# One decoder step on one core: an attention sum, a core's front and the DVE order moved, a K=100 product in place of two of four rows, and output products in two column halves

## The reference

```
block 1: u = rmsnorm(x) @ w_in
         o_a = rwkv7(u_rwkv)            # 8 heads of 64, a state recurrence over the tokens
         o_b = diff_attention(u_attn)   # 4 heads: softmax(q1 k1) - lam * softmax(q2 k2), times v, then
                                        # o * rsqrt(mean(o*o)) over the head's 128 columns
         x += (g_a * (o_a @ w_a) + g_b * (o_b @ w_b)) @ w_out
         x += relu(rmsnorm(x) @ w_ff1)^2 @ w_ff2 ; x += (p @ w_ple) * sigmoid(rmsnorm(x) @ w_ple_gate)
block 2: linear attention, 4 heads of 128 x 256, chunks of 64 tokens:
         o = (q k^T, causal in the chunk) v + q S      # S: the state at the chunk's start
         dilated attention, 3 groups x 4 heads, each with out_g and lse_g:
         w_g = softmax over g of lse_g ; o = sum_g w_g * out_g
         then gates, out projection, MLP and the per-layer embedding as in block 1
```

## Time and profile before

| | |
|---|---|
| three runs | 1974.45, 1980.01, 1980.01 us; median 1980.01 |
| the profiled execution | 1975.9 us, span 1974.1 |
| PE busy | 1933.8 us, 98% |
| DVE, ACT, POOL busy | 50%, 39%, 15% |
| mean granted clock of PE | 0.994 of full |
| transfers | 185.70 MB, mean 94 GB/s |

### The profile page before, as it was taken

The page is one execution under the profiler, slowest core; times in us unless marked ns, Lnnn a source line. Parts: engine busy times, 40 slices in busy tenths (PEclk is TensorE's granted clock), DMA queues, the critical chain, the costliest instruction groups (busy, mean ns, idle before and its releaser), DMA issues.

```text
span 1974.1 us, 27695 instructions
## 1 busy us (share of the span) xinstructions
PE 1933.8 (98%) x11560; PEld 1576.5 (80%) x11560; DVE 978.8 (50%) x1550; ACT 777.8 (39%) x1260; POOL 289.0 (15%) x281
## 2 busy tenths in 40 slices
PE   8989999999999999999999999999999999999997
PEld 6866777778888888887787888887888888888886
DVE  6655766657432333367645344447533432333365
ACT  6555323244443332346333333344222443232345
POOL 1001233302210010122000000004201210010124
PEclk9999999999999999999999999999999999999999
DMA  5122111135233322234312122222222242223221
GB/s 198 64 69 70 66 55 61 56 123 186 82 117 118 109 96 99 93 107 136 110 54 71 68 75 86 77 84 75 96 96 95 88 150 96 98 95 102 93 94 54
DMA packets 60080, 185.70 MB, mean 94 GB/s; under 512 B 6595, under 2 KB 11843, under 8 KB 59828
## 3 DMA queue, kind: packets, MB, share of 16 engines
q1 hardware_dynamic: 59956, 183.94, 27.7%
HBM read 173.69 MB, written 10.22 MB: 93 GB/s over the span
## 4 chain that ended last, share of the span: by engine, by line
PE 84%; DVE 7%; ACT 4%; issue 2%; POOL 2%; DMA 1%; SPq 0%; DVEq 0%; POOLq 0%; ACTq 0%
PE P L571 25%; PE P L573 24%; PE P L572 24%; DVE AREN L1763 2%; POOL AREN L2497 1%; DVE AREN L1766 1%; DVE WLO L1770 1%; ACT WHI L1171 1%; ACT AREN L1475 1%; PE P L1100 1%; PE P L1066 1%; PE P L760 1%; PE P L907 1%; PE P L919 0%; PE P L923 0%
## 5 line engine op out<-in xcount | busy, mean ns | idle before, releaser
L571 PE MATMUL P<-HH,WHI 128*128 128x512 f32 x1528 | 614.3, 402 | 5.3 <-DVE HL L1783 3.4
L573 PE MATMUL P<-HH,WLO 128*128 128x512 f32 x1528 | 597.6, 391 | 0.0
L572 PE MATMUL P<-HL,WHI 128*128 128x512 f32 x1528 | 596.9, 391 | 0.0
L1171 ACT ACTIVATE WHI<-RAW 128x1024 fp32r<-128x1024 f32 x302 | 318.1, 1054 | 432.5 <-PE P L573 431.6
L1770 DVE TENSOR_TENSOR WLO<-RAW,WHI 128x1024 fp32r<-128x1024 f32 x302 | 376.7, 1248 | 146.2 <-ACT WHI L1171 144.7
L571 PE MATMUL P<-ARR,WHI 128*128 128x512 f32 (+1 forms) x920 | 353.3, 384 | 0.0
L572 PE MATMUL P<-ARR,WHI 128*128 128x512 f32 (+1 forms) x920 | 352.8, 384 | 0.0
L573 PE MATMUL P<-ARR,WLO 128*128 128x512 f32 (+1 forms) x920 | 352.8, 384 | 0.0
L571 PEld LDWEIGHTS P<-HH,WHI 128*128 128x128 f32 x1528 | 287.8, 188 | 77.3 <-issue 7.9
L573 PEld LDWEIGHTS P<-HH,WLO 128*128 128x128 f32 x1528 | 287.6, 188 | 61.9
L572 PEld LDWEIGHTS P<-HL,WHI 128*128 128x128 f32 x1528 | 288.2, 189 | 55.8 <-issue 0.2
(11 more groups left out here) (311 smaller groups left out, 1444.2 us busy)
## 6 DMA issues: line engine op xcount, KB each, us to landing
RAW<-in_w_in_dram SPq DMA_DIRECT2D x117, 512.0 KB, 3.3
RAW<-in_w_ff_dram SPq DMA_DIRECT2D x64, 512.0 KB, 3.3
RAW<-in_w_ml_dram SPq DMA_DIRECT2D x64, 512.0 KB, 3.3
RAW<-in_w_out_dram SPq DMA_DIRECT2D x16, 512.0 KB, 3.3
RAW<-in_w_pg_dram SPq DMA_DIRECT2D x16, 512.0 KB, 3.3
AREN<-in_xT_dram SPq DMA_DIRECT2D x16, 256.0 KB, 6.0
s_gates<-AREN SPq DMA_DIRECT2D x16, 256.0 KB, 2.0
RAW<-in_w_ab_dram SPq DMA_DIRECT2D x8, 512.0 KB, 3.3
```

Of the source, the lines that this page charges most:

```text
L571: e.matmul(out, hi, H[0][:, s], start=first, stop=False)
L572: e.matmul(out, hi, H[1][:, s], start=False, stop=False)
L573: return e.matmul(out, lo, H[0][:, s], start=False, stop=last)
L1171: e.activation(WHI[n % NSPL][:, :], RAW[n % NRAW][:, :], ACT.Copy).then_inc(*D.act.sig("whi", n))
```

## The change

Five edits. `ss` of head h-1 now stands behind `aw` of head h (rows 77, 103, 129). front(0)'s first chunk moves to rows 182, 189, 192, 194, and front(1)'s to 196, 200, 203, 205. DVE's add to Q moves, for levels 1 to 4, from the `c` streams to the `e` streams, so that DVE's order after an `lb` is T0, T1, Q0, Q1. Linear attention does all 8 score products of a head first (one wait for both banks), then the 14 state products, each cut in two of 64 weight columns that write the two halves of the partitions. The log sums are turned by f32 transposes; the two fp32r parts lie in one buffer at partitions 0 to 3 and 96 to 99, the rest of which POOL sets to zero in the `l` stream, and EYE has a second copy of the identity at rows 96 to 99, so that one product of K=100 does what two of K=4 did.

```diff
     for h in range(4):
...
-            out += [("pv", h - 1, 0)] if h and i == 1 else [("ss", h - 1, 0)] if h and i == 5 else []
+            out += [("pv", h - 1, 0)] if h and i == 1 else []
             out.append(("qk", h, i))
         out.append(("aw", h, 0))
+        out += [("ss", h - 1, 0)] if h else []
...
-        put("a", r, r, r, *((r,) if late else ()), r + 3, r + 3, r + 3, *((r + 3,) if late else ()), r + 6, r + 6,
-            r + 11, *((r + 13,) if r < 117 else ()), r + 21, r + 21, r + 21, r + 21)
+        put("a", r, r, r, *((r,) if late else ()), r + 3, r + 3, r + 3, r + 6, r + 6, r + 11,
+            *((r + 12,) if late else ()), *((r + 13,) if r < 117 else ()), r + 21, r + 21, r + 21, r + 21)
...
-    for jj, rows in ((0, (174, 178, 181, 184)), (1, (196, 199, 202, 205))):
+    for jj, rows in ((0, (182, 189, 192, 194)), (1, (196, 200, 203, 205))):
...
-        EYE = sb("EYE", 4, F32R, 4)
+        EYE = sb("EYE", 4, F32R)
...
-        dLS = [(arr(28 + g)[0:4, :], arr(31 + g)[0:4, :]) for g in range(3)]
+        dLS = [(arr(28 + g)[0:4, :], arr(28 + g)[96:100, :]) for g in range(3)]
...
+                    w.wait_ge(G.dve.at("at", h, 1), G.dve.at("s", h, 7), free.get(4), free.get(5))
                     for vb in range(2):
...
+                            for x, rw in enumerate(rws):
+                                d = e.matmul(bank(4 + vb)[rw, 64 * c:64 * c + 64],
+                                             gST[:, c, 128 * vb + 64 * x:128 * vb + 64 * x + 64],
+                                             q[:, 64 * c:64 * c + 64], start=False, stop=c == 7)
...
-                        d = e.matmul(o[0:4, 128 * qb:128 * qb + 128], LSE[:, 16 * g + 4 * qb:16 * g + 4 * qb + 4],
-                                     ident, start=True, stop=True)
+                        d = e.transpose(o[0:4, 128 * qb:128 * qb + 128], LSE[:, 16 * g + 4 * qb:16 * g + 4 * qb + 4], ident)
...
-                        for i_ in range(2):
-                            d = e.matmul(o, EYE[0:4, h:h + 1].to_broadcast([4, 128]), dLS[g][i_], start=i_ == 0,
-                                         stop=i_ == 1)
+                        e.matmul(o, EYE[0:100, h:h + 1].to_broadcast([100, 128]), arr(28 + g)[0:100, :], start=True,
+                                 stop=True).then_inc(*L.pe.sig("mix", h, g))
...
+                    if what == "lb" and lev < 5:
+                        add(Qm, Qm, o0[:, 128:384]).then_inc(*C.dve.sig("Q", q, lev))
...
-                        add(Qm, Qm, o0[:, 128:384] if lev < 5 else o0[:, 0:256]).then_inc(*C.dve.sig("Q", q, lev))
+                        else:
+                            add(Qm, Qm, o0[:, 0:256]).then_inc(*C.dve.sig("Q", q, 5))
...
+                w.wait_ge(L.pe.at("pv", 11), L.act.at("pt", 11, 0))
+                for g in range(3):
+                    e.memset(arr(28 + g).bitcast(F32), 0.0).then_inc(*L.pool.sig("lz", g))
```

More of the change, by code:

```diff
@@ L1056, in gla @@
                         yield
+                    w.wait_ge(G.dve.at("at", h, 1), G.dve.at("s", h, 7), free.get(4), free.get(5))
                     for vb in range(2):
[L1058 to L1061, removed]
                         for tb in range(4):
-                            e.matmul(o[:, 128 * tb:128 * tb + 128], gVT[:, tb, cs], gATv[:, tb, :], start=tb == 0,
-                                     stop=False)
+                            e.matmul(bank(4 + vb)[:, 128 * tb:128 * tb + 128], gVT[:, tb, 128 * vb:128 * vb + 128],
+                                     gATv[:, tb, :], start=tb == 0, stop=False)
+                    for vb in range(2):
                         for c in range(1, 8):
-                            d = e.matmul(o[:, 64 * c:64 * c + 64], gST[:, c, cs], q[:, 64 * c:64 * c + 64],
-                                         start=False, stop=c == 7)
+                            for x, rw in enumerate(rws):
+                                d = e.matmul(bank(4 + vb)[rw, 64 * c:64 * c + 64],
+                                             gST[:, c, 128 * vb + 64 * x:128 * vb + 64 * x + 64],
+                                             q[:, 64 * c:64 * c + 64], start=False, stop=c == 7)
                         d.then_inc(*G.pe.sig("o", h, vb))
-                        free[b] = G.dve.at("o", h, vb)
-                        yield
+                        free[4 + vb] = G.dve.at("o", h, vb)
+                    yield
+                    yield
                     b, o = take(G.pool.at("sq", h))
@@ L1151, in dilated @@
                     for g in range(3):
-                        b, o = take(L.dve.at("ls", g), K.pool.at("eye"))
-                        for i_ in range(2):
-                            d = e.matmul(o, EYE[0:4, h:h + 1].to_broadcast([4, 128]), dLS[g][i_], start=i_ == 0,
-                                         stop=i_ == 1)
-                        d.then_inc(*L.pe.sig("mix", h, g))
+                        b, o = take(L.dve.at("ls", g), K.pool.at("eye", 1))
+                        e.matmul(o, EYE[0:100, h:h + 1].to_broadcast([100, 128]), arr(28 + g)[0:100, :], start=True,
+                                 stop=True).then_inc(*L.pe.sig("mix", h, g))
                         free[b] = L.dve.at("mix", h, g)
@@ L1734, in dilated @@
                     yield
-                w.wait_ge(L.dve.at("lw"))
+                w.wait_ge(L.dve.at("lw"), L.pool.at("lz", 2))
                 for g in range(3):
@@ L2525, in begin @@
                 e.tensor_copy(ONES[:, :], cst("ones")).then_inc(*K.pool.sig("one"))
-                e.tensor_copy(EYE[:, :], ident[0:4, 0:4]).then_inc(*K.pool.sig("eye"))
+                e.memset(EYE[:, :].bitcast(F32), 0.0).then_inc(*K.pool.sig("eye0"))
+                w.wait_ge(K.pool.at("eye0"))
+                for i, at in enumerate((0, 96)):
+                    e.tensor_copy(EYE[at:at + 4, :], ident[at:at + 4, at:at + 4]).then_inc(*K.pool.sig("eye", i))
+                w.wait_ge(K.pool.at("eye", 1))
                 for i in range(2):
```

## The result

The changed kernel takes 1960.87 us (median of four runs, 1960.29 to 1965.27), the kernel before, in the same rounds, 1978.48 (1974.45 to 1980.01). The ratio is 0.9919, with a 95% interval of 0.9897 to 0.9941: it is faster. Its profiled execution took 1961.4 us with a span of 1959.6, 14.5 under the span before.

A forecast was written before the change was run, and what follows sets the result against it. PE, busy 98% of the span, was taken as the bound. The terms summed to -17.0 us, from 1975.9 to 1958.9; half the difference between median and profiled execution was added, giving 1961, range 1952 to 1970.

The forecast's parts named there:

- Attention: Attention with `ss` moved: weights ready sooner, -2.6 us, a wait of about 3 us at row 117 staying.
- -0.9 of the later `pv`: Ahead of attention's `pv`: the later wait goes since head 3's weights are early, -0.9 us, between 0 and -1.2.
- -1.0 for the clock: Behind the wait at row 117: half rate again but for less, -1.0 us, between 0 and -2.7.
- Fronts: front(0)'s wait and half-rate stretch go, 6.5 us; a new 1.1 us wait at front(1): -5.4, bounds -3.5 and -6.5.
- T and Q: Cores, DVE's adds: core 0 may wait 0.36 us longer, no gain seen; +0.3 us, from 0 to +3.
- Linear attention: Linear attention's outputs: half-array products at 0.035 us each, 1.0 us per head, -4.0 for four, bounds -3.6 and -4.8.
- Rival E: Linear attention: halves do not overlap, each instruction takes 0.109 us, 16.2 us worse than summed, 1977 us; chance 0.03.
- Log sums and spread: Log sums -0.9 us; spread -2.2 at third and fourth place, -0.3 at the first two, 0 for the clock.
- C: Row 117, second spread place, front(1): new waits bring new half-rate stretches, two of 5.2 us; 1967 us, chance 0.23.
- A: Whole kernel: the terms come out as summed, 1961 us; chance 0.50.
- D: Attention and fronts: moved steps gain nothing because ACT's and DVE's chains set those places; 1971 us, chance 0.07.
- B: Clock stays up behind row 117, no new front wait, spread gives its full -5.9 us; 1955 us, chance 0.17.

The follow-up runs named there:

- third run: Kernel before with attention's sums of squares alone moved behind `aw`: 1973.2 us beside 1980.0.
- fifth: Changed kernel with the places of the spread at rows +72, +84, +92, +100 in place of +72, +80, +88, +96: 1955.0 us beside 1980.4.
- tenth: Changed kernel with DVE's add to Q as before the change and the spread at +72, +84, +92, +100, front(1) as in the change: 1957.31 us, ratio 0.9889.
- sixth run: Changed kernel with front(1)'s first chunk at rows 195, 201, 203, 205 in place of 196, 200, 203, 205: 1962.1 us beside 1980.4.
- fourth run: Changed kernel with DVE's adds in the old order T0, Q0, T1, Q1: 1959.4 us beside 1980.0.
- seventh run: Changed kernel with linear attention's 28 state products ordered 14 on the lower 64 partitions, then 14 on the upper, in place of taking turns: 1965.7 us beside 1980.4.
- first run: Kernel before with linear attention's outputs alone in the new form: 1971.8 us beside 1980.0.
- ninth: Kernel before with only the log sums turned by transposes and one product of K=100 in place of two of K=4: 1975.5 us beside 1980.4.
- second: Kernel before with the fronts' rows alone moved: 1974.8 us beside 1980.0.
- eighth: Changed kernel with DVE's old add to Q, the spread at +72, +84, +92, +100 and front(1) at 195, 201, 203, 205: 1956.83 us, ratio 0.9887.
- eleventh: The kernel with old add to Q, later spread and front(1) at 195, 201, 203, 205, plus attention's last head 3 rows later: 1953.58 us, ratio 0.9873.

## Why the prediction was right, and where it was not

The time came out at 1960.87 where 1961 was forecast. That closeness is partly luck: the trace gained 14.5 where the sum had 17.0, and the 2.1 us that were added for runs slower than the profiled one were not there, as the changed kernel's median lies 0.5 below its profiled execution.

**Attention.** Shown as forecast. PE comes to row 117 2.35 us sooner and waits 2.9 for copies that start at 113.73, 2.8 sooner than the earlier trace rows; DVE's waits for line 1491 fell from 11.5 us in four to 1.3 in one. The -0.9 of the later `pv` is -1.1. The -1.0 for the clock was right for this execution and is not the edit's: the third run has the wait without the shorter stretch, the fifth and tenth have the wait and no stretch at all.

**Fronts.** -4.1 for -5.4. The step that failed in size is the new wait at front(1)'s product, 1.95 us for the 1.1 taken, just above the 0.4 to 1.9 given for it. DVE was named rightly as what is late next, and its work was counted in full: from the end of the block ahead of it to front(1)'s keys it does 19 instructions before and after (the window begins where the split that was at 180.06 ends):

```profile
176.82:190.14 13.32, 12.70 (x55) 9.84 (x53) 11.26 (x19) 6.17 (x9) 2.06 (x2) 1.00 0.34 118
```

What was too small is the time between them. DVE needs 13.32 us, 1.4 more than the 11.90 of the earliest date, where the forecast counted about 0.7 of the 1.5 for round trips. From the keys to the product it takes 191.47 - 190.14 = 1.3 us and not 0.9, and PE comes to it 0.3 later than forecast. One of the 19 is a weight split of 1.64 us right ahead of the keys, and the sixth run shows that it can stand behind them. What went is 7.0 by row 184 less 0.7 for front(0)'s own steps in their new place, so 6.3 for the 6.5 of the sum; another 0.2 is lost between rows 200 and 208. Moving the split shows the second bound: the same chain of DVE then holds up the cores, and only 0.8 can be had.

**T and Q.** +0.9 for +0.3, of which 0.74 are the order's by the fourth run. The mechanism was the one named, the sign was right, and three places at 0.22 and one at 0.10 are inside the bound of 0 to 3.

**Linear attention.** -4.6 for -4.0. The row of rwkv's output gave 0.035 for an instruction; here one takes 0.032 with the way out, and 56 x 0.003 = 0.17 a head is the difference. Rival E, no overlap, is excluded by the seventh run, which also shows what it would have cost at this shape, 0.051 and not 0.109.

**Log sums and spread.** -1.05 for -0.9, and -1.0 for -2.5. The forecast saw the wait at the second place (2 to 3 us, measured 2.4), and put nothing down for the clock behind it. This is the step that failed: in this execution the stretch at half rate stands behind the second place and not behind the first, and it takes 0.8 us of the 1.0 that the third place gains. The fourth place gained its whole 1.0. The first two gave nothing (+0.2 for -0.3).

But the edit doesn't move the stretch, as the other traces show. The first run has the old spread. Its stretch stands behind the second place, after a wait of 2.05, and its rows 1552 to 1600 take 1.59 us more than in the trace of before. The fourth and seventh runs have the new spread. Their stretch stands behind the first place, as in the trace of before, the wait at the second place is 0.9, and the rows take 2.17 us less than there. The second place in PE's timelines of the first and of the fourth run:

```profile
1369.63 1.54 PE L1155 MATMUL P<-ARR,EYE 4*128 4x512 f32 x4 [2.05 <-DVE AREN L1764]
...
1361.29 1.10 PE L1155 MATMUL P<-ARR,EYE 100*128 100x512 f32 x2 [0.88 <-DVE AREN L1763]
```

With the stretch at the same place on both sides the edit is worth 2.2 us (fourth and seventh runs beside before) or 2.2 to 2.6 (ninth, sixth and changed kernel beside the first run). The -2.5 was near this; what it lacked is the 1.6 us by which the clock moves these rows, with the old spread as with the new.

**The rivals.** C, new waits with new half-rate stretches, came true in part: behind row 117 (3.4 us, shorter than before, as A had it) and at the second place of the spread, but with stretches of 3.4 us, where it was priced with two of 5.2. At front(1)'s product a wait of 1.9 to 2.0 was followed by none, in any of the six traces that have it. D is excluded by the second and third run. B wanted three things at once: the clock up behind row 117, which the fifth and tenth traces have by themselves; no wait at front(1), which no kernel with the change's rows has; and the full 5.9 of the spread, of which the fifth run with its later places has 4.9.

What stays open is when the clock falls. Up to row 117 the changed kernel and the fourth, fifth, sixth, seventh, eighth and tenth runs hold the same instructions and the same wait of 2.9, and behind it are 3.4, 3.4, 0, 6.8, 3.4, 3.4 and 0 us at half rate. From none to 6.8 is 2.6 us in PE's time at row 118, as large as most edits here. What sets these seven apart was not found, and no run was made for it.

## What to carry to other kernels

When a step is moved to where its input is ready, read what its own queue does between it and the next step of that kind: here DVE's queue, in which one weight split of 1.6 us could as well stand behind the step, set the next wait, and not the data. Making PE's work shorter ahead of a place that another engine dates turns the gain into a wait and perhaps into slow products behind it; the place has to move with the work, and four rows gave 1.4 to 3.9 us beyond the cheaper product. Before a stretch at half rate goes into a sum, look in several traces whether it stands at that place without the edit: here the same rows took 1.6 us more or less by it. To judge an edit of 1 to 3 us where single executions differ by 2.6 through the clock, compare the starts of the same row in two traces on both sides of the edit, and not the spans.

## What the runs showed of the hardware

The half-rate stretches do not belong to a place of the program. The same instructions brought none, one of 3.4 or one of 6.8 us behind row 117, and two executions (the seventh and the eleventh) had one behind row 360, where the other eleven traces have none; these two have the longest waits at that row, 1.81 and 2.32 us. The Trainium skill, "TensorE: Matmul & The Clock Gate", Part 1, tells of a kernel whose number of slow matmuls at its start differs from run to run. Here the same holds in the middle of a kernel, with 0 to 2.6 us for one wait.

One of the two instructions of an f32 product with 64 weight columns and 64 moving ones costs 0.051 us when the products of one half follow each other and 0.032 when the halves take turns (seventh run and changed kernel).

Twelve f32 transposes of 4 columns took the place of 24 product instructions, and eight of them last 1315.65 - 1314.86 = 0.79 us, 0.10 each: a transpose costs about as much as one of the two instructions of a product, 0.11.
